# Token-major weight panels reordered to contiguous 256-column runs, and large buffers moved to multiples of 1024 bytes

## The reference, cut to what matters

```python
mq, mk, mv, mo, mi, mf, sq, sk, sv = _split(h @ w_in, AB_SIZES)   # first mixer
...
q = (h @ wq); k = (memn @ wk); v = (memn @ wv)                    # cross attention, twice
...
proj = h @ w_in_even[i]      # fq, fk, fv, ff, dq, ckv, dkr, iq, ik, iw
...
mq, mk, mv = jnp.split(h @ w_in_odd[i], 3, axis=-1)
```

## Time and profile before

| | us |
|---|---|
| median of 3 runs | 1671.57 |
| lowest and highest of them | 1668.38, 1673.94 |
| the profiled execution, its own time | 1661.04 |
| its span, first to last instruction | 1659.3 |
| TensorE (PE) busy | 1583.7 |
| GpSimd (POOL) busy | 1190.6 |
| ScalarE (ACT) busy | 833.1 |
| VectorE (DVE) busy | 765.7 |

### The profile page before, as it was taken

One profiled execution on the slowest core, in us unless ns is written; L12 is line 12 of the kernel. 1 busy time (PEld: TensorE's weight loads), 2 busy tenths in 40 slices (PEclk: granted clock), 3 DMA queues, 4 the chain that ended last, 5 costly groups with the idle time before them and its releaser, 6 DMA issues. The chain is left out here.

```text
span 1659.3 us, 32586 instructions
## 1 busy us (share of the span) xinstructions
PE 1583.7 (95%) x12614; PEld 1508.7 (91%) x12614; DVE 765.7 (46%) x1392; ACT 833.1 (50%) x1252; POOL 1190.6 (72%) x920
## 2 busy tenths in 40 slices
PE   7989999999999899999999999989999998999997
PEld 6878989999998788998999998869999997899997
DVE  6647244220076656544422005955554228465521
ACT  4664455554465544555555445455545444555442
POOL 5654976988967600496699896806999997189995
PEclk9998999999999989999999999989999999899999
DMA  7332534555544300353455554305556553155552
GB/s 284 128 102 96 184 127 153 185 186 189 187 157 152 115 1 1 103 178 128 153 190 185 185 191 140 127 26 166 192 194 197 193 192 115 52 178 187 185 188 102
DMA packets 67662, 248.56 MB, mean 150 GB/s; under 512 B 7632, under 2 KB 7888, under 8 KB 67152
## 3 DMA queue, kind: packets, MB, share of 16 engines
q1 hardware_dynamic: 67536, 246.71, 44.8%
HBM read 245.63 MB, written 1.05 MB: 149 GB/s over the span
## 5 line engine op out<-in xcount | busy, mean ns | idle before, releaser
L343 POOL TENSOR_TENSOR ring_lo<-ring,ring_hi 128x512 fp32r<-128x512 f32 x916 | 1190.4, 1335 | 449.3 <-ACT ring_hi L987 446.9
L987 ACT ACTIVATE ring_hi<-ring 128x1024 fp32r<-128x1024 f32 x458 | 465.9, 1051 | 203.9 <-DMA ring<-panels 195.9
L377 PE MATMUL ps_dve<-x_hi,ring_hi 128*128 128x256 f32 x1928 | 468.5, 281 | 15.7 <-POOL ring_lo L343 10.9
L377 PE MATMUL ps_dve<-x_lo,ring_hi 128*128 128x256 f32 x1928 | 464.1, 279 | 0.0
L377 PEld LDWEIGHTS ps_dve<-x_hi,ring_hi 128*128 128x128 f32 x1928 | 362.2, 188 | 21.9 <-issue 15.0
L377 PEld LDWEIGHTS ps_dve<-x_lo,ring_hi 128*128 128x128 f32 x1928 | 362.3, 188 | 0.5 <-issue 0.2
L377 PE MATMUL ps_dve<-x_hi,ring_lo 128*128 128x256 f32 x1928 | 275.6, 279 | 0.0
L377 PEld LDWEIGHTS ps_dve<-x_hi,ring_lo 128*128 128x128 f32 x1928 | 247.2, 188 | 0.8 <-POOL ring_lo L343 0.6
L377 PE MATMUL ps_dve<-work_parts,ring_hi 128*128 128x256 f32 x1728 | 231.7, 279 | 0.0
L377 PEld LDWEIGHTS ps_dve<-work_parts,ring_hi 128*128 128x128 f32 x1728 | 217.1, 188 | 0.0
L1472 DVE TENSOR_TENSOR xT<-xT,ps_dve 128x512 f32<-128x512 f32 x40 | 27.5, 688 | 336.6 <-PE ps_dve L377 336.6
(11 more groups left out here) (272 smaller groups left out, 2023.5 us busy)
## 6 DMA issues: line engine op xcount, KB each, us to landing
ring<-panels SPq DMA_DIRECT2D x458, 512.0 KB, 3.3
consts<-constants SPq DMA_DIRECT2D x1, 2208.0 KB, 12.7
xT<-x_t SPq DMA_DIRECT2D x1, 1024.0 KB, 5.0
memn<-mem_t SPq DMA_DIRECT2D x1, 1024.0 KB, 19.1
out_t<-xT SPq DMA_DIRECT2D x4, 256.0 KB, 2.3
smalls<-small_operands SPq DMA_DIRECT2D x1, 824.5 KB, 15.7
consts<-constants SPq DMA_DIRECT2D x1, 129.5 KB, 4.9
angle_i<-positions SPq DMA_DIRECT2D x1, 128.0 KB, 7.9
```

Source lines behind the costliest of these rows:

```text
L343: pool.tensor_tensor(ring_lo[:, s, cs], ring[:, s, cs], plain(ring_hi[:, s, cs]), ALU.subtract).then_inc(sem("lo_made"), 1)
L377: ins = pe.matmul(o, lhsT, rhs, start=start, stop=stop, skip_group_check=True)
L987: tell(act.activation(ring_hi[:, n % RING, :], ring[:, n % RING, :], ACT.Copy), "hi_made")
```

## The change

It does three things.
1. Two unused buffers are put in: 224 columns (896 bytes) ahead of `ring_hi`, and 240 columns (960 bytes) ahead of `xT`. With the rounding, `ring_hi`, `ring`, `xT`, `x_hi`, `x_lo`, `memn`, `sq`, `scratch`, `mixT` and `work` then all start on a multiple of 1024 bytes.
2. On the host, the blocks of the 36 token-major panels are put in another order: of two neighbouring panels, the first now holds k = 0 to 3 for 256 columns and the second k = 4 to 7, and the 256 columns of one k are a contiguous run of 1024 bytes.
3. `project_tokens` uses the panels one at a time. Per panel it waits for that panel's high part, does 8 high matmuls for tokens 0 to 127 and 8 for the others, then the 8 low ones in order of k, waiting for each half's count on its own (`low_ready`), and gives the panel back. The number of matmuls and of weight loads stays as it was, 48 for two panels.

```diff
+        sb("ring_margin", [P, 224])
         ring_hi = sb("ring_hi", [P, RING, PANEL * P], F32R)
...
         smalls = sb("smalls", [P, N_SMALL])
+        sb("stream_margin", [P, 240])
         xT = sb("xT", [P, C, T])
...
                 for p in range(n_banks):
                     o = bank(who, freed_by)
-                    n = state["block"] // PANEL
-                    state["block"] += 2 * PANEL
-                    s = n % RING
-                    hi, lo = (r[:, s:s + 2, :].rearrange("p m (k c) -> p m k c", c=P) for r in (ring_hi, ring_lo))
-                    pe.wait_ge(sem("hi_made"), n + 2)
-                    for t in range(TT):
-                        half = o[:, t * T:(t + 1) * T]
-                        ts = slice(t * P, (t + 1) * P)
-                        for k in range(C):
-                            mm(half, src[0][:, k, ts], hi[:, :, k, :], k == 0, False)
-                            mm(half, src[1][:, k, ts], hi[:, :, k, :], False, False)
-                        if t == 0:
-                            pe.wait_ge(sem("lo_made"), 2 * (n + 2))
-                        for k in range(C):
-                            end = t == TT - 1 and k == C - 1
-                            state["used"] += 2 if end else 0
-                            mm(half, src[0][:, k, ts], lo[:, :, k, :], False, k == C - 1, who if end else None)
+                    for first in range(0, C, PANEL // 2):
+                        n = state["block"] // PANEL
+                        state["block"] += PANEL
+                        s = n % RING
+                        pe.wait_ge(sem("hi_made"), n + 1)
+                        for t in range(TT):
+                            half, ts = o[:, t * T:(t + 1) * T], slice(t * P, (t + 1) * P)
+                            for k in range(PANEL // 2):
+                                w = ring_hi[:, s, k * T:(k + 1) * T]
+                                mm(half, src[0][:, first + k, ts], w, first + k + t == 0, False)
+                                mm(half, src[1][:, first + k, ts], w, False, False)
+                        for k in range(PANEL // 2):
+                            low_ready(n, 2 * k)
+                            for t in range(TT):
+                                half, ts = o[:, t * T:(t + 1) * T], slice(t * P, (t + 1) * P)
+                                end = first + k == C - 1
+                                state["used"] += t == TT - 1 and k == PANEL // 2 - 1
+                                mm(half, src[0][:, first + k, ts], ring_lo[:, s, k * T:(k + 1) * T], False, end,
+                                   who if end and t == TT - 1 else None)
...
+    by_token = {"ab_in": ((8, 12), (16, 20)), "even_in": ((18, 22),), "odd_in": ((16, 24),),
+                "xv0": ((0, 8),), "xv1": ((0, 8),)}
...
+        for first, last in by_token.get(name, ()):
+            tok = b[first * C:last * C].reshape(-1, 2, C, P, P)
+            b[first * C:last * C] = tok.transpose(0, 2, 1, 3, 4).reshape(-1, P, P)
```

## The result

The changed kernel takes 1685.35 us (median of 4 runs, 1682.70 to 1686.09) against 1669.97 us of the kernel before (4 runs, 1667.11 to 1673.94). The ratio is 1.0088, with an interval of 1.0062 to 1.0113: **slower by 0.9%**, some 15 us, where 0.4% faster was forecast and 1676 us was the top of the range. The profiled execution took 1682.70 us.

A forecast was written before the change was run, and what follows sets the result against it. TensorE, busy in 95% of the span, was taken to bound the kernel. The seven pauses gave 6.3 us and all other terms zero, so the median 1671.57 - 6.3 = 1665.3 us, with a range of 1610 to 1676.

The forecast's parts named there:

- What bounds the kernel: Whole kernel: TensorE, busy in 95% of 1659.3 us; only fewer pauses or a shorter distance between its matmuls save time.
- Matmuls, loads, bytes: Whole kernel: nothing added or removed, 18 banks x 48 matmuls with the same loads, copies, subtractions and transfers; cost zero.
- Single use of panels: Token-major banks: a bank no longer waits for both panels, so seven pauses go; gain 0 to 6.3 us, 6.3 taken.
- Waits by halves: Token-major panels: one added wait per panel between the fourth and fifth low matmul, up to 0.9 us a time; taken as zero.
- One run instead of two, and multiples of 1024 bytes: Weight matmuls: joined runs and aligned starts likeliest change nothing; ends 37.7 us gained, or 11.7 plus 49.5 us lost.
- The prediction's own last sentence: Long stretches of matmuls: if every one has one pace, whichever it is, the forecast is wrong and the addresses did choose.
- Rival 3: Weight matmuls: both streams starting on a multiple of 1024 collide, each paying one more step of 4.5 ns; 1716 us, chance 0.10.
- The sum against the profiled executions: Whole kernel: the profiled execution of 1661.0 us less 6.3 gives 1654.7 us.
- The rule on lines of 16 bytes: SBUF accesses: consecutive ones inside a 16-byte line run at full bandwidth, so alignment and joining of runs give nothing.
- The 109.2 ns: Matmuls of 256 columns: estimate from N / 2.4 + 2.5 ns; neither pace seen before the change agreed with it.

The follow-up runs named there:

- margins_only: The kernel before with the two unused buffers put in and nothing else, panels still used in pairs: 1692.75 us, ratio 1.0137 to the kernel before.

## Why the prediction was wrong

**What bounds the kernel**: right. TensorE is busy 96% of the span after the change, and the time moved with its pace. **Matmuls, loads, bytes**: right, the counts are equal.

**Single use of panels**: right, in mechanism and in size. 6.3 us were forecast; with the margins out of the way it measured 0.49%, 8.2 us of 1667.51 (3.7 to 12.5 by the interval), and no idle time is left before the token-major matmuls. That the size came out so near is in part luck, since the interval is as wide as the gain. **Waits by halves**: zero was right, no new wait shows.

**One run instead of two, and multiples of 1024 bytes**: this step failed. It took zero, and the margins measured a loss of 1.37%, about 23 us (13.7 to 32.2). Three readings in it went wrong.
- "Where buffers start cannot alone choose the pace", because two paces occur at the same addresses. True, but it does not follow that the addresses do nothing: they set *which* paces exist. At distance 64 there are two, which a pause or a change of operands can switch; at distance 0 there is one of 120.0 ns, and no pause or change of operands in these traces leads out of it.
- Blocks with odd and even k start at the same step. I took that as a test of crossing a multiple of 1024, and it is one. But the property that counts repeats every 256 bytes, and k moves the starts by 512 or 1024 bytes, so this comparison could not see it.
- The 2 ns of duration between the slow paces of token-major and feature-major were seen and left without a consequence. They were the trace of a second distance inside the kernel.

The prediction's own last sentence named the sign of this error: every long stretch has one pace, so the addresses did choose.

**Rival 3**, both streams starting at the same place, named the cause and the direction, but its step was mis-sized: it charged 4.5 ns more than the slow pace, and the runs show 120.0 - 117.8 = 2.2 ns. Its "against", that token-major has another offset and the same quick pace, was the same error as above. Its deciding point, a feature-major stretch above 118.3 ns, was passed. With the measured step the sum would have been 1672.7 + 10,992 x 2.2 ns - 6.3 = 1690.6 us, and 1685.35 was measured; the chance given to it, 0.10, was too small.

**The sum against the profiled executions.** The mean step before was 0.24 x 113.3 + 0.76 x 117.8 = 116.7 ns, so 120.0 costs 10,992 x 3.3 ns = 36.3 us; less 6.3 for the pauses that is 30.0, and the spans differ by 21.6. The two traces say where the rest is. The weight matmuls were busy 1299.7 us and are busy 1334.0, 34.3 more (they overlap with the others by 15 us in both). TensorE's idle time fell by 6.9, near the 6.3. The other 1646 matmuls, whose work is the same, were busy 299.0 us and are busy 293.2, 5.8 less: 34.3 - 6.9 - 5.8 = 21.6. Those 5.8 us go with TensorE's clock. It was granted 0.986 of full on average instead of 0.980, so (0.020 x 1659.3 - 0.014 x 1680.9) x 2 = 19 us less were spent at 1.2 GHz, the lower of its two levels. That the clock gave all of the 5.8 us was not tried.

**The rule on lines of 16 bytes** ("SBUF — State Buffer" of the Trainium skill, cited in the prediction) does not agree with these runs as far as it was stretched there. All starts in the sweep are multiples of 16 and all runs contiguous, and the pace moved from 113.3 to 120.0 ns. The Trainium skill also says in "TensorE: Matmul & The Clock Gate", in its steps of a matmul, that the moving operand and the weight load have read ports of their own, so that loading the next tile takes no read bandwidth from the running matmul. The measurement differs: the two do not run free of each other here, since the pace moved by 6.7 ns with their distance, with all other engines and transfers idle too. Whether they meet at a port or behind it no run tells. The 109.2 ns that the prediction estimated from the formula of the Trainium skill was reached at no distance; the page gives that formula for an isolated matmul, and says that in a stream of load and matmul pairs both set the spacing, so it was no bound for this kernel.

## What to carry to other kernels

Where TensorE loads a new stationary operand for every matmul of 256 columns of 4 bytes, treat the byte distance between its two operands as a tuning parameter: read the step from starts over many matmuls, sweep one buffer's start in steps of 32 bytes over 256 (the grid used here), and do not expect round addresses to be best. Here one number, `stream_margin` of 32 columns with no `ring_margin`, makes the changed kernel 1.1% quicker than the kernel before (interval 0.3 to 2.0%) instead of 0.9% slower. And when two durations differ by 2 or 3 ns in a row of thousands of matmuls, ask what sets them before calling their cause zero.

## What was not expected of the hardware

- The step of a matmul with its weight load depends on moving start less stationary start, modulo 256 bytes as far as 0 with 256 and 192 with 448 show it: 120.0 ns at 0, mostly 113.3 at 192. The sign matters. At distances 0, 64 and 192 the paces are the same with every other engine idle.
- At distances 64, 192 and 448 two steady paces exist, 113.3 and 117.8 ns, at the same granted clock, in different shares. What picks one is not known. In the kernel before, all three unpaused changes from slow feature-major into token-major (163.6, 701.6 and 1060.9 us) turned slow into quick; a break of 0.28 us between two starts at 1160 us turned slow into quick, and the pause before 710.08 us quick into slow.
- Part of why runs of one kernel scatter may be these shares: the kernel before took 1652.60 to 1675.72 us over 19 runs of one session. This was argued, not measured run by run, and it cannot be all of it: at distance 0, with its single pace, the changed kernel took 1682.70 to 1686.09 us over 4 runs, but `margins_only` 1684.26 to 1698.06.
- What repeats every 256 bytes, and why 96 is as slow as 0, no run here tells. The distances between multiples of 32, and places of the weights other than 0 and 128, were not tried. Nor was distance 192 in a kernel that uses its panels in pairs.
